# Hybrid decoder step on one core: the dilated prompt attention and the SSD prompt stage merged into one slotted stage, with the x part of the convolution on GpSimd

## What is computed

```python
def dilated_prompt(q, k, v, rel_bias):          # three groups g, dilations 1, 4, 16
    ...
        def block(i):                           # 128 queries, 2 heads of 64
            ...
            return dilated_attend(qb, jnp.take(kw, local, axis=1), jnp.take(vw, local, axis=1), bias, valid)

def ssd_mixer(z, xbc, dt_raw, conv_buf, h0, conv_w, conv_b, dt_bias, A_log, D_skip, norm_w):
    xbc_c = jax.nn.silu(causal_dwconv(xpad, conv_w, conv_b))      # 4 taps over 896 channels
    xs, Bm, Cm = jnp.split(xbc_c, [C_INNER, C_INNER + C_GROUPS * C_STATE], axis=-1)   # 384, 256, 256
    ...
    y, h_new = ssd_scan(xs, dt, A, Bm, Cm, h0.astype(F32))        # 16 chunks of 128 positions
    y = y + D_skip.astype(F32)[:, None] * xs
    y = y.reshape(b, T, C_INNER) * jax.nn.silu(z.astype(F32))
```

## Time and profile before

| | |
|---|---|
| median of 3 runs | 3884.94 us |
| the profiled execution: its own time | 3885.07 us |
| its span in the trace | 3883.4 us |
| mean granted TensorE clock | 0.907 of full |
| PE busy | 3193.3 us (82%) |
| DVE, ACT, POOL busy | 1603.3, 830.1, 657.1 us |
| dilated stage, first DMA issue to that of the next stage | 1221.2 to 1444.6 us |
| SSD prompt stage, likewise | 1444.6 to 1796.8 us |

### The profile page before, as it was taken

One profiled execution on the slowest core, in us unless ns is written; L12 is line 12 of the kernel. 1 busy time (PEld: TensorE's weight loads), 2 busy tenths in 40 slices (PEclk: granted clock), 3 DMA queues, 4 the chain that ended last, 5 costly groups with the idle time before them and its releaser, 6 DMA issues. The chain is left out here.

```text
span 3883.4 us, 47996 instructions
## 1 busy us (share of the span) xinstructions
PE 3193.3 (82%) x16985; PEld 2716.7 (70%) x16985; DVE 1603.3 (41%) x2894; ACT 830.1 (21%) x1465; POOL 657.1 (17%) x406
## 2 busy tenths in 40 slices
PE   4799689779997758883068769999999599999997
PEld 3688579656664547773057668989989478787886
DVE  2112132257783433443433244544544534344444
ACT  2111111123332432220022221211211222121211
POOL 0000000024441112220022121211211022121120
PEclk8899899889997758996589989999999799999998
DMA  6422432277761221112343340111110321111111
GB/s 249 166 97 91 139 127 79 59 202 209 203 188 52 57 67 40 44 44 91 88 137 135 137 172 33 44 54 33 47 51 11 138 86 54 43 45 53 33 43 49
DMA packets 193028, 358.31 MB, mean 92 GB/s; under 512 B 72855, under 2 KB 113496, under 8 KB 186954
## 3 DMA queue, kind: packets, MB, share of 16 engines
q1 hardware_dynamic: 152899, 257.59, 21.5%
q10 hardware_dynamic: 36032, 67.68, 4.7%
q0 software_dynamic: 4016, 32.05, 2.5%
HBM read 290.92 MB, written 95.49 MB: 100 GB/s over the span
## 5 line engine op out<-in xcount | busy, mean ns | idle before, releaser
L2358 PE MATMUL cm_g_ps<-cm_h_hi,cm_up_hi 128*128 128x344 f32 (+1 forms) x880 | 312.0, 355 | 124.2 <-POOL cm_up_lo L2197 90.8
L2359 PE MATMUL cm_g_ps<-cm_h_lo,cm_up_hi 128*128 128x344 f32 (+1 forms) x880 | 309.8, 352 | 0.0
L2360 PE MATMUL cm_g_ps<-cm_h_hi,cm_up_lo 128*128 128x344 f32 (+1 forms) x880 | 309.5, 352 | 0.0
L2358 PE MATMUL cm_u_ps<-cm_h_hi,cm_up_hi 128*128 128x344 f32 (+1 forms) x880 | 306.9, 349 | 0.0
L2359 PE MATMUL cm_u_ps<-cm_h_lo,cm_up_hi 128*128 128x344 f32 (+1 forms) x880 | 305.6, 347 | 0.0
L2360 PE MATMUL cm_u_ps<-cm_h_hi,cm_up_lo 128*128 128x344 f32 (+1 forms) x880 | 305.6, 347 | 0.0
L2202 POOL TENSOR_TENSOR cm_dn_lo<-cm_dn_raw,cm_dn_hi 128x1024 fp32r<-128x1024 f32 x44 | 107.7, 2470 | 1002.7 <-ACT cm_dn_hi L2234 1002.7
L2358 PEld LDWEIGHTS cm_g_ps<-cm_h_hi,cm_up_hi 128*128 128x128 f32 x880 | 167.8, 191 | 147.5 <-issue 133.2
L2197 POOL TENSOR_TENSOR cm_up_lo<-cm_up_raw,cm_up_hi 128x2048 fp32r<-128x2048 f32 x44 | 204.2, 4643 | 285.4 <-ACT cm_up_hi L2219 285.4
L288 PE MATMUL pja_acc<-pja_w_hi,pja_h_hi 128*128 128x480 f32 (+1 forms) x512 | 198.4, 387 | 61.3 <-DVE pja_h_lo L225 61.3
L2225 ACT ACTIVATE cm_gate<-cm_g_ps 128x344 f32<-128x344 f32 (+1 forms) x110 | 55.1, 511 | 806.4 <-PE cm_g_ps L2360 805.5
(11 more groups left out here) (451 smaller groups left out, 7093.1 us busy)
## 6 DMA issues: line engine op xcount, KB each, us to landing
fp_kv<-in_fox_kv SPq DMA_DIRECT2D x256, 256.0 KB, 3.0
cm_up_raw<-in_w_up SPq DMA_DIRECT2D x44, 1024.0 KB, 4.9
cm_dn_raw<-in_w_down SPq DMA_DIRECT2D x44, 512.0 KB, 3.6
out_s_win<-in_cache POOLq DMA_DIRECT2D x1, 16376.0 KB, 32.1
proj_a<-pja_row ACTq DMA_DIRECT2D x17, 962.0 KB, 4.1
proj_b<-pjb_row ACTq DMA_DIRECT2D x17, 643.0 KB, 3.3
sp_raw<-proj_b SPq DMA_DIRECT2D x16, 640.0 KB, 4.0
dp_raw<-proj_a POOLq DMA_DIRECT2D x48, 192.0 KB, 3.3
```

The source lines that it names most:

```text
L2358: pe.matmul(out, hi, h_hi[:, k, cs], start=(k == 0), stop=False)
L2359: pe.matmul(out, hi, h_lo[:, k, cs], start=False, stop=False)
L2360: last = pe.matmul(out, lo, h_hi[:, k, cs], start=False, stop=(k == KT - 1))
```

## The change

`dilated_prompt` and `ssd_prompt` become one function, `local_stage`, written out without loops in SLOTS = 55 slots. Three slots make a chunk of the SSD, and each slot begins one unit of the attention. In slot s, with phase s % 3, the chunk `now` = s // 3 is brought in and convolved and the chunk `back` = now - 1 is scanned; unit s - 2 is transposed, s - 3 scored, s - 4 turned, s - 5 multiplied with its values and s - 6 stored. `unit(s, step)` and `chunk(s, back, phase)` say which. Every engine walks the slots in the order that its own loop gives.

Further: the x tiles (384 of the 896 channels) are convolved by POOL in eight operations of 128x384 (`convolve_x`), and the four B and C tiles by PE, one in phase 1 and three in phase 2. q and k of a unit are copied by one ACT operation (`copy_qk`), the two heads' scores are issued apart (`score(u, 0)`, `score(u, 1)`), SP issues all loads and stores, `sT` is formed in two halves, and the gates of a chunk are read in place where before they were copied to `a_now` (L1572). The PSUM banks are shared: three for the attention, five for the SSD.

```diff
-def dilated_prompt(nc, pa, consts_d, rel_d, onehot_d, toep_d, ma, raw_landed):
-def ssd_prompt(nc, pb, consts_d, conv_d, conv_rows_d, heads_d, gates, mc, p_ssm_d, p_conv_d):
...
+def local_stage(nc, pa, pb, consts_d, rel_d, onehot_d, toep_d, conv_d, conv_rows_d, heads_d, gates, ma, mc,
+                p_ssm_d, p_conv_d):
+
+    UNITS = GROUPS * TILES
+    LAG = 2
+    SLOTS = UNITS + LAG + 5
+    RAWS, OUTS, BANKS = 8, 6, 3
...
+            return 0 < u < TILES or (TILES <= u < 2 * TILES and u % 4 > 0)
+
+        def unit(s, step):
+            u = s - LAG - step
+            return u if 0 <= u < UNITS else None
+
+        def chunk(s, back, phase):
+            c = s // 3 - back
+            return c if s % 3 == phase and 0 <= c < TILES else None
+
...
+            def convolve_x(c):
+                pool.wait_ge(in_ready, 2 * c + 1)
+                pool.wait_ge(halo_ready, c + 1)
+                if c >= 1:
+                    pool.wait_ge(s_ready, 2 * c - 1)
+                def tap(j):
+                    return taps[:, 0:XT, j:j + 1].to_broadcast([P, XT, P])
+
+                gps.link(pool, pool.tensor_tensor(x_conv[:], xT[:, c % 2, 0:XT, 0:P], tap(0), ALU.mult))
+                gps.link(pool, pool.tensor_tensor(x_conv[:], x_conv[:], tap(C_CONV), ALU.add))
+                for j in range(1, C_CONV):
+                    gps.link(pool, pool.tensor_tensor(x_part[:], xT[:, c % 2, 0:XT, j:j + P], tap(j), ALU.mult))
+                    last = pool.tensor_tensor(x_conv[:], x_conv[:], x_part[:], ALU.add)
+                    if j < C_CONV - 1:
+                        gps.link(pool, last)
+                last.then_inc(x_conv_ready, 1)
+
+            pool.wait_ge(setup, 64)
+            pool.wait_ge(gates_a, 1)
...
+                if c is not None:
+                    pool.wait_ge(decay_ready, c + 1)
+                    pool.wait_ge(cb_ready, c + 1)
+                    if c >= 1:
...
+                    last.then_inc(mix_ready, 1)
+                    if c >= 1:
+                        pool.wait_ge(y_ready, c)
+                    pool.tensor_tensor(skip[:], xs[:], heads[:, 1].unsqueeze(2).to_broadcast([P, H, HD]), ALU.mult
...
+                if c is not None:
+                    mask(c)
+                c = chunk(s, 0, 1)
+                if c is not None:
+                    convolve_x(c)
+
...
+            for s in range(SLOTS):
+                u = unit(s, 3)
+                if u is not None:
+                    copy_out(u)
+                c = chunk(s, 1, 0)
+                if c is not None:
+                    act.wait_ge(x_turned, c + 1)
...
+                if c is not None:
+                    act.wait_ge(seg_done, c + 1)
+                    if c >= 2:
+                        act.wait_ge(mix_ready, c - 1)
+                    for g in range(C_GROUPS):
+                        last = act.activation(decay[:, c % 2, g * HG:(g + 1) * HG].rearrange("p h n -> p (h n)"),
+                                              seg_ps[:, g], ACT.Exp)
+                    last.then_inc(decay_ready, 1)
...
+                if u is not None:
+                    exps(u)
+                c = chunk(s, 0, 0)
+                if c is not None:
...
+                    for b in range(2):
+                        lo, hi = 4 * b, min(4 * b + 4, CT)
+                        act.activation(xT[:, c % 2, lo:hi, C_CONV - 1:], m_ps[:, b, 0:(hi - lo) * P].rearrange(
+                            "p (c n) -> p c n", n=P), ACT.Copy).then_inc(in_ready, 1)
...
+                    act.wait_ge(x_conv_ready, c + 1)
+                    if c >= 1:
+                        act.wait_ge(s_ready, 2 * c - 1)
+                    act.activation(tanh[:, 0:XT], x_conv[:], ACT.Tanh).then_inc(tanh_ready, 1)
+                    act.wait_ge(conv_done, 2 * c + 2)
+                    if c >= 1:
+                        act.wait_ge(s_ready, 2 * c)
+                    act.activation(tanh[:, XT:].rearrange("p c n -> p (c n)"), conv_ps[:, XT * P:CT * P], ACT.Tanh
+                                   ).then_inc(tanh_ready, 1)
+                c = chunk(s, 1, 2)
+                if c is not None:
+                    act.wait_ge(y_ready, c + 1)
+                    if c >= 1:
+                        act.wait_ge(squared, c)
+                    act.activation(sq_junk[:], y_out[:, c % 2, 0:C_INNER], ACT.Square,
+                                   accum_out=y_out[:, c % 2, C_INNER:MIX_C]).then_inc(squared, 1)
+                u = unit(s, 0)
+                if u is not None:
...
+            def activate(c, half):
+                lo, hi = (XT, CT) if half else (0, XT)
+                v.wait_ge(tanh_ready, 2 * c + half + 1)
+                if c >= 2:
+                    v.wait_ge(st_done, c - 1)
+                pre = conv_ps[:, XT * P:CT * P].rearrange("p (c n) -> p c n", n=P) if half else x_conv[:]
+                v.scalar_tensor_tensor(out=sT[:, c % 2, lo:hi], in0=tanh[:, lo:hi], scalar=1.0, in1=pre,
+                                       op0=ALU.add, op1=ALU.mult).then_inc(s_ready, 1)
...
+            for s in range(SLOTS):
+                now, back = s // 3, s // 3 - 1
+                u = unit(s, 1)
+                if u is not None:
+                    score(u, 0)
+                u = unit(s, 3)
+                if u is not None:
+                    value(u)
+                u = unit(s, 2)
+                if u is not None:
+                    turn_p(u)
+                u = unit(s, 1)
+                if u is not None:
+                    score(u, 1)
+                if s % 3 == 0:
+                    if 0 <= back < TILES:
+                        turn_x(back)
+                    if now < TILES:
+                        turn_in(now)
+                if s % 3 == 1 and 0 <= back < TILES:
+                    turn_b(back)
+                if s % 3 == 2 and 0 <= back < TILES:
+                    states(back)
+                u = unit(s, 0)
+                if u is not None:
+                    turn(u)
+                if s % 3 == 0 and now < TILES:
+                    if now == 0:
+                        pe.wait_ge(gates_exp, 3)
+                    segments(now)
+                if s % 3 == 1 and now < TILES:
...
-        dilated_prompt(nc, pa, i["consts"], i["rel"], i["dist_prompt"], toep, ma, blocks_landed)
-        ssd_prompt(nc, pb, i["consts"], i["conv_cols"], i["conv_rows"], i["heads"], gates, mc, o["p_ssm"], o["p_conv"])
+        local_stage(nc, pa, pb, i["consts"], i["rel"], i["dist_prompt"], toep, i["conv_cols"], i["conv_rows"], i["heads"],
+                    gates, ma, mc, o["p_ssm"], o["p_conv"])
```

More of the change, by code:

```diff
@@ L1346, in sb @@
         def sb(name, shape, dt=F32):
[L1347 to L1350 removed]
+            return ctx.enter_context(nc.sbuf_tensor(name, shape, dt))
         def sem(name):
[L1353 to L1357 removed]
@@ new lines, in local_stage @@
+        z_tanh = sb("sp_z_tanh", [P, C_INNER])
+        xs = sb("sp_xs", [P, H, HD])
+        xd = sb("sp_xd", [P, H, HD])
+        xdd = sb("sp_xdd", [P, H, HD])
+        skip = sb("sp_skip", [P, H, HD])
+        b_tok = sb("sp_b_tok", [P, C_GROUPS, C_STATE])
+        a_mask = sb("sp_a_mask", [P, H, P])
+        decay = sb("sp_decay", [P, 2, H, P])
+        cb = sb("sp_cb", [P, C_GROUPS, P])
+        mix = sb("sp_mix", [P, H, P])
+        state = sb("sp_state", [P, 2, H, HD])
+        y = sb("sp_y", [P, 2, H, HD])
@@ new lines, in _ @@
+            for s in range(SLOTS + 2):
+                if 3 <= s + 1 < UNITS:
+                    load_blk(s + 1)
+                c = chunk(s, -1, 0)
+                if c is not None and c >= 2:
+                    load_raw(c)
+                u = unit(s, 4)
+                if u is not None:
+                    store_blk(u)
+                c = chunk(s, 2, 0)
+                if c is not None:
+                    sp.wait_ge(squared, c + 1)
+                    sp.dma_start(mc[(c + 1) * P:(c + 2) * P, :], y_out[:, c % 2]).then_inc(stored[c % 2], 16)
@@ L1540, in _, with copy_out, exps @@
-            act.sem_inc(squared, 1)
-            over_chunks(act, ahead, body)
-            act.wait_ge(stored[0], 16 * 9)
-            act.wait_ge(stored[1], 16 * 9)
+            def copy_out(u):
+                act.wait_ge(pv, u + 1)
+                act.activation(out[:, u % OUTS, 0:P], w_ps[:, u % BANKS, 0:P], ACT.Copy).then_inc(o_ready, 1)
+            def exps(u):
+                act.wait_ge(max_ready, u + 1)
+                if u >= 2:
+                    act.wait_ge(p_turned, u - 1)
+                lo = 0 if before(u) else P
+                for h in range(2):
+                    last = act.activation(probs[:, u % 2, h, lo:], s_sb[:, u % 2, h, lo:], ACT.Exp, scale=SCALE,
+                                          bias=neg[:, u % 2, h:h + 1], accum_out=out[:, u % OUTS, P + 2 + h:P + 3 + h])
+                last.then_inc(exped, 1)
@@ L1565, in _ @@
+            last.then_inc(diag_ready, 1)
             v.wait_ge(gates_exp, 3)
[L1567 to L1579 removed]
```

(2 more changed lines are left out.)

857 lines of the change are left out of this document (386 added, 471 removed).

## The result

The changed kernel takes 3927.24 us, the median of 4 runs (3919.72 to 3937.88), against 3885.70 us for the kernel before in the same set. The ratio is 1.0099, with a 95% interval of 1.0056 to 1.0142: 1% slower. The profiled execution took 3919.72 us, 34.7 us more than the one of before.

What follows compares the result with a forecast made beforehand. A slot-by-slot chain between engines, with PE's clock changing, was taken as the bound: 37.7 us a chunk with blocks before, 33.2 without, 545 us plus prologue and last scan, 30 us over the profiled 3885.07, giving 3915; range 3805 to 3985.

Steps and rivals of the forecast that it cites:

- What holds PE between slots: End of phases 0 and 2: the next slot's first score waits for ACT's late q and k copy; 3.4 us in phase 0.
- Slots A and B at a changing clock: A (phase 0): 7 us at the low clock, 9.1 plus 3.4 waiting; B (phase 1): low up to `cb`, 7.1 us.
- POOL's chain: From `cb` on, POOL does `mix`, `skip` and eight x convolution operations, holding ACT: 12.0 us a chunk, 7.7 for the convolution.
- the exclusion: POOL and DVE exclude each other in some operations beside POOL's chain: 1.5 us a chunk.
- What ends a chunk: Phases 1 and 2: POOL's chain, then a 5.1 us tail end the chunk; PE's 15.2 us at the high clock end earlier.
- C: Phase 2 of a chunk: clock low for 5 us; its tail of tanh, `sT`, y operations, square and copy takes 5.1 us.
- the sum: Merged stage: 37.7 us a chunk with blocks before, 33.2 without; 545 us for 15 chunks.
- the second rival: Merged stage: clock stays low and PE bounds phase 2; 46.4 and 38.5 us a chunk, 4030 us in all; chance 0.15.
- The prologue: Start of the merged stage, 1221.2 to about 1254 us: constants, distance table, gates, then slots 0 to 2.
- The clock staying high: Rival for the merged stage: PE keeps the high clock; 30.3 and 27.4 us a chunk, 3811 us in all; chance 0.17.
- Busy times: Rival for the merged stage: waits hidden, PE at the high clock; 20.8 and 17.1 us a chunk, 3665 us; chance 0.06.
- slot A would stay low: Phase 0, 14 transposes for 8 to 16 records: by the skill's rule its clock stays low, as in the second rival.

Runs made afterwards that it cites:

- the fastest kernel: Changed kernel with q and k copied early, the second half of `sT` before the operations on y, and `a_mask` in phase 0 behind `xdd`: 3688.99 us, ratio 0.9508.

## Why the prediction came out as it did

The forecast was 3915 us, within 1% of the kernel before, and the range 3805 to 3985; measured were 3927. The time was right, and one of its steps was not.

*What holds PE between slots.* Right. ACT's copy ended PE's waits, 2.82 and 3.07 us long (3.4 was forecast for phase 0), and the runs with the early copy show what hangs on them.

*Slots A and B at a changing clock.* Right: in the chunk shown the clock rose 8.8 us into A (7 forecast) and was low again in B. A took 12.8 us from score to score (12.5 forecast), and from there to `cb` it took 7.06 us (7.1).

*POOL's chain.* Its length was over-estimated a little: from the mix to the end of the convolution 10.98 us, where I had 12.0. The convolution took 8.0 (7.7 forecast); DVE held POOL up in one operation a chunk, mostly by 0.33 us, not by 1.5 in all. The other way round the exclusion is real: `sT` took 1.25 in place of 0.56 us beside the mask, as forecast. The Trainium skill (SBUF — State Buffer, section on its two separate sides) says that whichever of the two starts first holds the SBUF ports that they share for its whole instruction; 1252 against 558 ns agrees, for the mask had started first (1405.70 against 1406.33).

*What ends a chunk.* This is the step that failed. "PE's own work in B and C, 15.2 us at the high clock [...] ends before that", and "1 for PE being late in C when the clock is low": PE was late in 15 of the 16 chunks, by 8.1 to 8.8 us of DVE's waiting in six of them and by 0.6 to 4.3 in nine. From `cb` to the next slot A the chunk shown took 24.5 us, where the sum had 12.0 + 5.1 + 1. I had let the clock rise 5 us into C. In the first chunks it stayed low through all of C (28.6 us at 0.50), later it rose in C: a chunk took 37.4 us at 0.68. That was the second rival's mechanism, with its place and its point, and it made chunks of 44.3 us where that rival had 46.4. I had given it 0.15 and counted it for all chunks or none.

*Why the sum still came out.* From slot 3's first score (1249.0) to slot 48's (1808.3) it took 559.3 us for 545 forecast. The first eleven chunks took 39.7 us each, not 37.7, and the four without 30.6, not 33.2, since there the clock was better than I took it. Errors of both signs partly cancelled, which was luck; the clock was forecast as one mean course, and it came as three kinds of chunks. The prologue was right to a microsecond (32.0 us to slot 3, 32.8 forecast). The stage grew by 44.7 us and the rest of the program took 10 less, of which the change explains nothing.

*The rivals.* The clock staying high would have given 3811 in the late order; twelve useless products at each gap come near this, with 3799. Busy times gave 3665 for no waiting at all: the fastest kernel comes to 3689. What was said against this case, that each slot's first score waits for ACT's last operation, was exactly what the early copy took away.

*Transposes.* The Trainium skill (TensorE: Matmul & The Clock Gate, section on the PE-mode transpose) says that they don't count as busy in the same way. I had read from it that slot A would stay low; it didn't, for the clock rose in its segment sums. In the fastest kernel every slot A has 14 and more transposes, and the clock is 0.98 over 316 us. If the rule holds, the work around them is enough.

## What to carry to other kernels

When two stages are merged into slots, look on every engine at what the next slot's first instruction needs, and put that ahead of everything in its slot that waits: here one copy of 0.4 us behind other work was worth 200 us. Price a gap on PE at more than its length, above all behind a stretch that has just raised the clock: in this kernel the gaps of 42 and 45 us in all cost 71 and 134 us, and useless products in them made the program faster. Moving work to a slower engine pays only as long as that engine is not in the chain: it brought 135 us where PE was the bound at the low clock, and 26 where the copy was early and POOL's chain took over.

## What was not expected of the hardware

PE worked for 28.6 us without a gap at a clock of 0.50, and with one gap of 3.1 us in 41 us it stayed at 0.54 for four chunks (151.71 us busy of 164). The changed kernel, with late copies and twelve useless products at each gap, ran at 0.94. The clock rose within the segment sums of phase 0 in the early chunks, and not in the 28.6 us of scores, values, transposes, convolution and outputs behind them; why there is open. In the kernel before it was alike: 19 us of unbroken convolution at 0.50, which I had read and not carried over to slot C, where three tiles of convolution are 8 of PE's 19 us. There, too, the clock rose within segment sums: they ran from 1483.00 to 1485.31 us, and the granted clock was 0.50 up to 1484.5 and 1.00 from 1485.0.

POOL's operation with a broadcast operand went from 0.83 to 1.16 us in one place in most chunks, beside one DVE operation with two inputs that had started 0.07 us earlier, and DVE's from 0.56 to 1.25 us beside one POOL operation of 1.47 that had started 0.63 us earlier (both in the chunk shown). In both the one that started second took longer, so an operation on POOL that can lie anywhere belongs where DVE is quiet.
